# Sixteen gathers of the last tile made in two parts, of 120 and of 8 tokens

## What is computed

```python
def block(xb):                       # 128 tokens
    ...                              # 8 heads x 16 best experts of 16384: eid, and their gates g
    u = jnp.take(u_tab, eid, axis=0)
    act = jax.nn.gelu(jnp.einsum('thkd,td->thk', u, xb))
    return jnp.einsum('thk,thkd->td', g * act, jnp.take(v_tab, eid, axis=0))
```

## Time and profile before

| what | value |
|---|---|
| median of 3 runs | 1901.11 us (1900.4 to 1903.69) |
| the profiled execution, its own time | 1903.1 us |
| its span, first to last instruction | 1900.5 us |
| VectorE busy | 1477.6 us |
| TensorE busy | 1447.2 us |
| gathers (POOL DMA_INDIRECT) | 512, 555.78 MB on their queue |

### The profile page before, as it was taken

The page is one execution under the profiler, slowest core; times in us unless marked ns, Lnnn a source line. Parts: engine busy times, 40 slices in busy tenths (PEclk is TensorE's granted clock), DMA queues, the critical chain, the costliest instruction groups (busy, mean ns, idle before and its releaser), DMA issues.

```text
span 1900.5 us, 15786 instructions
## 1 busy us (share of the span) xinstructions
PE 1447.2 (76%) x4603; PEld 844.4 (44%) x4603; DVE 1477.6 (78%) x2803; ACT 509.1 (27%) x1429; POOL 899.3 (47%) x658
## 2 busy tenths in 40 slices
PE   8999998999878887878777777668655555655554
PEld 4465587878635555545454234334321111211111
DVE  1645359993696778988977788879889889898877
ACT  3200130122332244222412432223322222222222
POOL 0778613340354444433434355436655555555651
PEclk9999999999989998989898798878887777777776
DMA  8434311135799999999999999999999999999995
GB/s 325 168 122 166 109 70 67 69 114 238 281 388 422 421 421 421 421 421 421 421 420 421 400 420 421 421 409 420 421 421 421 422 422 422 421 421 422 422 422 234
DMA packets 91082, 650.42 MB, mean 342 GB/s; under 512 B 10477, under 2 KB 10869, under 8 KB 12789
## 3 DMA queue, kind: packets, MB, share of 16 engines
q0 software_dynamic: 76448, 555.78, 70.9%
q1 hardware_dynamic: 13520, 90.25, 12.1%
q10 hardware_dynamic: 1029, 3.39, 0.5%
HBM read 647.26 MB, written 2.11 MB: 342 GB/s over the span
## 4 chain that ended last, share of the span: by engine, by line
DMA 40%; PE 28%; DVE 21%; issue 6%; ACT 3%; POOL 2%; DVEq 0%; SPq 0%; ACTq 0%; POOLq 0%
DMA arena<-in_peer_uv,arena 40%; PE bank L840 12%; DVE arena L1994 7%; PE bank L1141 5%; DVE arena L2030 5%; PE bank L1029 3%; POOL arena L772 2%; PE bank L795 2%; PE bank L877 1%; PE bank L954 1%; ACT arena L1448 1%; DVE arena L1957 1%; DVE arena L1749 1%; PE bank L966 1%; PE bank L816 1%
## 5 line engine op out<-in xcount | busy, mean ns | idle before, releaser
L772 POOL DMA_INDIRECT arena<-in_peer_uv,arena x512 | 700.8, 1369 | 731.7 <-DVE arena L2030 438.5
L1141 PE MATMUL bank<-arena,smalls 128*128 128x512 f32 x1052 | 664.5, 767 | 418.8 <-ACT smalls L1456 418.8
L1994 DVE CUSTOM_DVE_ANT_0 arena<-arena 128x1024 f32<-128x1024 f32 x512 | 619.0, 1222 | 159.5 <-DMA arena<-in_peer_uv,arena 158.2
L1141 PEld LDWEIGHTS bank<-arena,smalls 128*128 128x128 f32 x1052 | 221.0, 228 | 786.7 <-ACT smalls L1456 592.9
L2030 DVE SCALAR_TENSOR_TENSOR arena<-arena 128x1024 f32<-128x1024 f32 x243 | 310.4, 1278 | 37.4 <-ACT arena L1448 34.8
L840 PE MATMUL bank<-arena 128*128 128x256 f32 (+1 forms) x1216 | 334.5, 432 | 4.3 <-ACT arena L1206 3.9
L1443 ACT ACTIVATE arena<-arena 128x2 f32<-128x2 f32 x255 | 51.9, 203 | 926.9 <-DVE arena L1994 926.8
L840 PEld LDWEIGHTS bank<-arena 128*128 128x128 f32 x1216 | 235.1, 195 | 104.5 <-issue 78.8
L1448 ACT ACTIVATE arena<-arena 128x1 f32<-128x1 f32 x510 | 122.5, 287 | 8.6
L1084 PE MATMUL bank<-arena 128*128 128x256 f32 x480 | 108.5, 379 | 0.0
L1456 ACT ACTIVATE smalls<-ident,arena 128x128 f32<-128x128 f32 x263 | 104.7, 401 | 8.3
(11 more groups left out here) (270 smaller groups left out, 1294.3 us busy)
## 6 DMA issues: line engine op xcount, KB each, us to landing
arena<-in_w_in SPq DMA_DIRECT2D x40, 1024.0 KB, 5.6
arena<-in_w_ada POOLq DMA_DIRECT2D x16, 1024.0 KB, 5.1
arena<-in_w_out SPq DMA_DIRECT2D x16, 1024.0 KB, 9.0
arena<-in_peer_w_q SPq DMA_DIRECT2D x16, 1024.0 KB, 9.3
arena<-in_w_ada SPq DMA_DIRECT2D x8, 1024.0 KB, 10.6
arena<-in_peer_uv,arena POOLq DMA_INDIRECT x512, 19.4
arena<-in_x SPq DMA_DIRECT2D x4, 512.0 KB, 12.0
arena<-row_scratch ACTq DMA_DIRECT2D x1, 2048.0 KB, 9.1
```

What stands on the lines that cost most here:

```text
L772: nc.gpsimd.indirect_dma_start(gslot[slot], None, uv_tab[0], bass.IndirectOffsetOnAxis(eid[t % 2][:, k:k + 1], 0)).then_inc(s_gsl[slot], 16)
L1141: last = mm(acc[h][:, :], diag[:, k % NDG], row_v(n)[:, h * 512:(h + 1) * 512], start=first, stop=last_one)
L1994: V.tensor_tensor_reduce(row_u(n), row_u(n), h2[t], 1.0, 0.0, ALU.mult, ALU.add, dots[:, k:k + 1]).then_inc(s_dot, 1)
```

## The change

Of the gathers of tile 3, those numbered 400, 406, 412 and so on to 490 (`cut_rows`, sixteen of them) are issued as two: one for tokens 0 to 119 with the indices where they were, and one for tokens 120 to 127. For the second the eight tokens' indices are read from a new tile, `eidx`, in which they lie on partitions 0 to 7. SyncE fills it with four small transfers (`shift_ids`, 8 partitions by 32 columns, 1 KB each), each after the ranking of its 32 columns is done; GpSimd waits for the one that it needs ahead of a cut gather. Both parts add 16 to the slot's semaphore, so such a gather counts as two uses. Nothing else is changed: slots, order and the work of the other engines are as before.

```diff
+    CUT = 120
+    cut_rows = set(range((LT - 1) * NE + 16, NPK - 16, 6))
...
-        uses[slot] = uses.get(slot, 0) + 1
+        uses[slot] = uses.get(slot, 0) + 1 + (n in cut_rows)
...
+        eidx = sb("eidx", [P - CUT, PH * TOP], U32)
...
+            def shift_ids(q4):
+                lo = q4 * 2 * TOP
+                sp.wait_ge(s_eid, (LT - 1) * QB + q4 + 2)
+                sp.dma_start(eidx[:, lo:lo + 2 * TOP], eid[(LT - 1) % 2][CUT:P, lo:lo + 2 * TOP]).then_inc(s_eidx[q4], 16)
+
             for t in range(LT - 1):
+                if t == LT - 2:
+                    shift_ids(0)
                 sp.wait_ge(s_fin, t + 1)
                 sp.dma_start(out[0, t * P:(t + 1) * P, :], x1t[t]).then_inc(s_out[t // NA], 16)
+            for q4 in range(1, QB):
+                shift_ids(q4)
...
+                if n in cut_rows:
+                    q4 = k // (2 * TOP)
+                    pool.wait_ge(s_eidx[q4], 16)
+                    nc.gpsimd.indirect_dma_start(
+                        gslot[slot][0:CUT], None, uv_tab[0], bass.IndirectOffsetOnAxis(eid[t % 2][0:CUT, k:k + 1], 0)
+                    ).then_inc(s_gsl[slot], 16)
+                    nc.gpsimd.indirect_dma_start(
+                        gslot[slot][CUT:P], None, uv_tab[0], bass.IndirectOffsetOnAxis(eidx[:, k:k + 1], 0)
+                    ).then_inc(s_gsl[slot], 16)
+                    continue
```

More of the change, by code:

```diff
@@ L486, in build @@
         s_gready, s_eid = sem("gates_ready"), sem("expert_ids_ready")
+        s_eidx = [sem(f"expert_ids{n}_shifted") for n in range(QB)]
         s_gsl = [sem(f"row{i}_landed") for i in range(NGS)]
```

## The result

The changed kernel takes **2001.95 us** in the median of 6 runs (1993.04 to 2009.41), the kernel before 1901.61 us (1900.4 to 1903.69, 6 runs). The ratio is 1.0522, 95% interval 1.05 to 1.0545: 100 us slower, where I had forecast 4.6 us faster. The profiled execution took 2009.41 us, its span 2007.3 us.

The account below looks back on a forecast made before the run. The prediction took DMA gathers to bound the kernel, one engine about 11 us behind most. Relief of 4.6 us, closing packets' 0.1 included, other terms zero, gave 1901.1 - 4.6 = 1896.5 us; 8 in 10 range 1894.5 to 1906.5.

Parts of the forecast that it names:

- What bounds the kernel: Late gathers: DMA engines at full rate, one about 11 us behind most others, setting the landing of every late gather.
- The step that failed: Cut gathers' bytes: same 1 MiB each, only the carrying engine can change; 0.31 us per packet, 4.6 us gained.
- Relief of the latest engine: Sixteen cuts take 128 packets, 39.7 us, from the engine of tokens 120 to 127, taken as the latest.
- My first rival: No net relief: the fifteen engines differ each time, or the eight tokens return to the same engine; 1901.2 us, chance 0.25.
- GpSimd, SyncE, the index transfers: Sixteen more GpSimd issues, 15 to 23 us, and four 1 KB index transfers, covered by waits and queued work: zero.
- The small closing packets: Sixteen more on every engine from the extra transfers: 0 to 4.3 us, taken as 0.1 us.
- the loose tokens: Tokens 120 to 127 of each cut go one each to eight engines: 16 packets, 5.0 us more for those.
- The upper end of this term: Closing packets at 4.3 us for sixteen; said to bring the forecast to 1900.8 us, within the range.
- The rivals on the slow side: Latest engine gets loose tokens: 1906.2 us, chance 0.10; loose tokens pile up on two or one: 1909.8 or 1929.7, 0.12.
- What would show it: Trace signs: if right, no engine alone over 2 us; otherwise long tails, or a DMA share gap near 1710 us.

Follow-up runs that it names:

- e8: Kernel before, but sixteen gathers bring only tokens 32 to 95, the others left out: 1882.99 us, ratio 0.9893.
- e1: Changed kernel with all gathers whole; only the four index transfers and GpSimd's waits for them stay: 1902.43 us, ratio 1.0001 to the kernel before.
- e6: Kernel of its own, gathers alone: nine streams of 60, whole or of chosen tokens; whole 152 us, tokens 32 to 95 78 us.
- e5: Kernel of its own, gathers alone: single ones, then seven streams of 60, some gathers cut or replaced; 120 + 8 takes 40 us more than whole.
- e9: Changed kernel with four of the sixteen cuts (gathers 400, 430, 460, 490): 1931.87 us, ratio 1.0152 to the kernel before.
- e10: Kernel before with only gathers 508 to 511 cut into 120 and 8, small gathers ahead to move the starting engine: 1914.46 us, ratio 1.0069.
- e11: Kernel before with only gathers 510 and 511 cut into 120 and 8, small gathers ahead to move the starting engine: 1909.78 us, ratio 1.004.
- stream 4: Gathers alone, 60 whole ones, eight of them followed by the last eight tokens once more to another place: 11.5 us more than all whole.
- e2: Changed kernel without the parts of eight tokens, so the sixteen gathers bring only tokens 0 to 119: 2005.53 us, ratio 1.0543 to the kernel before.

## Why the prediction was wrong, point by point

**What bounds the kernel** was read rightly: the DMA engines at their rate, and one engine behind the others. The two experiments in the kernel that left the packets' time alone moved it by the work left out (e8, -20 us), or not at all (e1). The completion records bear out the ends that I read from the shares: for gather 511 the latest engine has 1889.7 us, the second-latest 1880.7, the third 1879.3, and the others 1876.8 to 1878.5.

**The step that failed** is the first of the change: "What can change is which engine carries them." I priced a packet at 0.31 us whichever engine carries it, and then only counted packets, 16 here and 128 there. The runs show a second thing that can change, a packet's time. In e6 it is 0.31 us for tokens 32 to 95 and twice that for 0 to 63, with the same number of packets (401 against 207 GB/s); by theory A1 that is without and with another engine writing into the same group of partitions. In the changed kernel its mean is 0.45 us from 1600 to 1872 us, and that is the loss of 100 us. The row of the whole gather gave a packet's time only for the layout of a whole gather, and I had written myself that no row showed a gather of fewer tokens; an upper bound for the packet's time was missing.

**The size**, worked out from those runs: if each of 120 packets is written into a group whose own engine is always busy, two packets lose 0.31 us each: 120 x 0.62 / 16 = 4.7 us per cut. Gathers alone lose 5.0 (e5), the kernel 6.3 with sixteen cuts and 7.2 with four. That the place of the tokens makes the packets slow is shown by e6 to e8; that two packets lose 0.31 us each is a working assumption, and the sum an estimate. The packet records tell a little more. What the 8 KB packets took beyond their mean of 0.314 us in the kernel before, from 1550 us on and divided by 16 engines, is 105 us in the changed kernel, 6.6 us for each cut, 22 us in e9, and 0 in e1 and e8. The profiled execution of the changed kernel was 106 us longer than that of the kernel before. So with sixteen cuts the whole loss is in longer packets; with four they hold 22 of 29 us. Why they are lengthened more there than among gathers alone (4.3 us for each cut) is open.

**Relief of the latest engine**: not in fifteen of sixteen cuts. My first rival, no net relief because the fifteen engines begin elsewhere each time, was right in its mechanism (once in sixteen in two kernels, and with the start moved in e10 and e11), and its price of nothing was wrong for the same reason as the forecast. The Trainium skill's page "DMA: Bandwidth & Descriptors", section "Why a DMA increments its semaphore by 16 and not by 1", which I had weighed there, fits the trace: the latest engine's share was missing at the thirteenth cut alone (0.6 and 0.2 us in the table), as it would be with 120 tokens on fifteen engines from a moving start.

**GpSimd, SyncE, the index transfers**: zero each, and e1 shows zero. **The small closing packets**: 0.1 us for sixteen was not separately measured; e5's stream 4 shows 1.4 us for a small transfer of eight tokens with all that belongs to it, more than the 0.31 us that I gave the loose tokens. In the change it doesn't show on top: e2, without them, is no faster. The upper end of this term would have given 1900.7 us, not 1900.8, since 0.1 us of it was in the forecast already.

**The rivals on the slow side** had prices from 5 to 29 us. They too moved packets between engines at a fixed price, so none reached 100 us. **What would show it**: I named long tails and gaps in the share. The sign that came was another, a full share at a fallen rate.

## What to carry to other kernels

A DMA-bound stretch has two numbers, share and rate; where the share is full, a change that alters which engine writes where can cost rate without any idle time showing. Gathers to all 128 partitions ran at 0.31 us a packet, the least that any stream here showed; cutting some, even into 64 + 64, slowed them and the whole gathers beside them (503 to 507 in e10). If a part has to be gathered alone, place decides: 64 tokens at partition 32 ran at full rate, the same 64 at partition 0 or 64 at half.

## What the runs showed of the hardware that I had not expected

- A stream of gathers of 64 tokens ran at 207 GB/s to partitions 0 to 63 and at 206 to 64 to 127, and at 401 to 32 to 95, with 64 packets of 8 KB in each gather, and all sixteen engines busy (shares 1.01, 1.01 and 0.98).
- The engine that a gather of 120 tokens leaves out moves from cut to cut. At the thirteenth cut it was the latest engine, with steps of 23 and of 15; with the start moved to suit, it was that engine in the first three cuts of e10 and in both of e11. The fourth of e10, at 2.0 us, isn't clear.
- The latest engine stays the same one relative to the start in four kernels (the changed one, e2, e10 and e11). Whether its lag of some 11 us comes from the engine or from the tokens of the whole gathers that it serves isn't separated, and why it is late stays open.
- The loss of a cut is larger in the kernel (6.3 to 7.2 us) than among gathers alone (5.0 us). Longer packets hold it, as far as the sixteen cuts go; why they are longer there wasn't settled.
